# Backbone step on one core: prompt's input projection between the samples' passes, single loads, one-hot gates on the second one-hot

## What is computed

```python
def trunk_layer(x, cvec, ctx_kv, ...):
    shift1, scale1, gate1, shift2, scale2, gate2 = adaln(cvec, w_ada, b_ada)
    h = rmsnorm(x, g_attn) * (1 + scale1) + shift1
    zf, zq, zk, zv, zp = jnp.split(h @ w_in, IN_SPLITS, axis=-1)
    ...
    gf, ga, gp = jnp.split(jax.nn.sigmoid(h @ w_gate + b_gate), N_BRANCHES, axis=-1)
    x = x + gate1 * ((gf * branch_f + ga * branch_a + gp * branch_p) @ w_out)
    h2 = rmsnorm(x, g_ffn) * (1 + scale2) + shift2
    x = x + gate2 * peer_ffn(h2, peer_wq, peer_keys, peer_u, peer_v)

def peer_ffn(h, peer_wq, peer_keys, peer_u, peer_v):
    q = (h @ peer_wq).reshape(B, L, PEER_HEADS, 2, PEER_D_KEY // 2)
    s = jnp.einsum('blhpc,hpnc->blhpn', q, peer_keys)
    sv, si = lax.top_k(s, PEER_TOPK)
    ...
    eid = jnp.take_along_axis(cid, pos, axis=-1)
    act = jax.nn.gelu(jnp.einsum('tkd,td->tk', peer_u[ee], hh))
    return jnp.einsum('tk,tkd->td', gg * act, peer_v[ee])
```

## Time and profile before

| | us |
|---|---|
| median of three runs | 3088.42 (3085.93 to 3094.46) |
| the profiled execution | 3086.08 |
| its span, first to last instruction | 3083.8 |

### The profile page before, as it was taken

One profiled execution on the slowest core, in us unless ns is written; L12 is line 12 of the kernel. 1 busy time (PEld: TensorE's weight loads), 2 busy tenths in 40 slices (PEclk: granted clock), 3 DMA queues, 4 the chain that ended last, 5 costly groups with the idle time before them and its releaser, 6 DMA issues.

```text
span 3083.8 us, 42725 instructions
## 1 busy us (share of the span) xinstructions
PE 2616.6 (85%) x14564; PEld 2042.2 (66%) x14564; DVE 2236.8 (73%) x4292; ACT 1271.1 (41%) x2320; POOL 1282.3 (42%) x966
## 2 busy tenths in 40 slices
PE   5799788856799999999978988884579999999996
PEld 1476654315688888888867666432568888888885
DVE  0335564448699999999993544565868999999998
ACT  0333332106455555455543333211544555555553
POOL 0554621007544444444437455200754444444441
PEclk6799899958999999999989999997899999999998
DMA  9743447595799999999965334663579999999995
GB/s 329 250 150 100 145 168 244 196 336 153 264 366 376 353 375 356 362 376 367 367 248 184 107 135 145 207 227 109 157 260 353 375 362 376 368 373 379 367 377 188
DMA packets 262282, 842.73 MB, mean 273 GB/s; under 512 B 33488, under 2 KB 104848, under 8 KB 224528
## 3 DMA queue, kind: packets, MB, share of 16 engines
q1 hardware_dynamic: 177328, 567.09, 52.0%
q0 software_dynamic: 73728, 268.47, 21.6%
q10 hardware_dynamic: 11104, 5.82, 0.7%
HBM read 805.09 MB, written 39.95 MB: 274 GB/s over the span
## 4 chain that ended last, share of the span: by engine, by line
issue 36%; DVE 27%; DMA 16%; POOL 9%; DVEq 6%; ACT 2%; PE 2%; ACTq 1%; POOLq 1%; SPq 0%; PEldq 0%; PEld 0%
DMA raw<-in_experts 11%; POOL wlo L667 8%; DVE wlo L1992 8%; DVE u L1742 6%; DVEq L2025 5%; DVE u L2003 4%; DVE u L1981 4%; DMA raw<-in_w_ada 3%; DVE u L2013 3%; ACT whi L996 1%; ACTq L1084 1%; DVEq L1987 1%; PE acc L1151 1%; DVE u L1984 1%; DMA raw<-in_peer_wq 0%
## 5 line engine op out<-in xcount | busy, mean ns | idle before, releaser
L673 POOL DMA_INDIRECT u<-in_u_rows,rowid x256 | 474.1, 1852 | 904.4 <-DVE u L1742 716.9
L1992 DVE TENSOR_TENSOR wlo<-raw,whi 128x1024 fp32r<-128x1024 f32 x512 | 624.6, 1221 | 116.8 <-ACT whi L996 80.6
L1502 PE MATMUL aux<-lt_hi,whi 128*128 128x256 f32 x2048 | 606.5, 296 | 71.2 <-DVE wlo L1992 69.4
L996 ACT ACTIVATE whi<-raw 128x1024 fp32r<-128x1024 f32 x512 | 536.5, 1049 | 153.4 <-DMA raw<-in_experts 152.7
L1502 PE MATMUL aux<-lt_hi,wlo 128*128 128x256 f32 x2048 | 584.8, 286 | 0.0
L1502 PE MATMUL aux<-lt_lo,whi 128*128 128x256 f32 x2048 | 584.7, 285 | 0.0
L1502 PEld LDWEIGHTS aux<-lt_hi,whi 128*128 128x128 f32 x2048 | 396.4, 194 | 144.5 <-DVE wlo L1992 128.7
L667 POOL TENSOR_TENSOR wlo<-raw,whi 128x1024 fp32r<-128x1024 f32 x144 | 355.5, 2479 | 267.1 <-ACT whi L822 266.9
L1514 PE MATMUL acc<-whi,bt_hi 128*128 128x512 f32 x1024 | 405.8, 396 | 13.4 <-DVE bt_lo L2022 13.2
L1514 PE MATMUL acc<-wlo,bt_hi 128*128 128x512 f32 x1024 | 404.5, 395 | 0.0
L1514 PE MATMUL acc<-whi,bt_lo 128*128 128x512 f32 x1024 | 401.4, 392 | 0.0
(11 more groups left out here) (211 smaller groups left out, 3841.5 us busy)
## 6 DMA issues: line engine op xcount, KB each, us to landing
raw<-in_experts SPq DMA_DIRECT2D x256, 1024.0 KB
raw<-in_w_ada SPq DMA_DIRECT2D x96, 512.0 KB, 5.4
raw<-in_w_gate SPq DMA_DIRECT2D x48, 1024.0 KB, 5.1
raw<-in_w_in SPq DMA_DIRECT2D x32, 1024.0 KB, 5.3
raw<-in_peer_wq SPq DMA_DIRECT2D x32, 1024.0 KB, 5.1
gmat<-u SPq DMA_DIRECT2D x32, 1024.0 KB, 5.1
z<-gmat SPq DMA_DIRECT2D x32, 1024.0 KB, 8.5
raw<-in_w_out SPq DMA_DIRECT2D x16, 1024.0 KB, 5.0
```

The lines of the kernel that those rows point to most:

```text
L673: pool.indirect_dma_start(UROWS[:, j % UBUF, :], None, a["u_rows"], bass.IndirectOffsetOnAxis(ap=ROWID[:, j:j + 1], axis=0))\
L996: act.activation(whi[:, i % SLOTS], raw[:, i % SLOTS], ACT.Copy).then_inc(expert_hi, 1)
L1502: mm = pe.matmul(b[:, 0:TS], w[:, slot, c * P:(c + 1) * P], x[:, c, :], start=(c == 0 and i == 0), stop=(c == KC - 1 and i == 2))
L1992: dve.tensor_tensor(wlo[:, i % SLOTS], raw[:, i % SLOTS], whi[:, i % SLOTS].bitcast(F32), ALU.subtract)\
```

## The change

**PE order.** The prompt's 8 transposes stand ahead of the samples' wa, in0 between wa and out, in1 between out and q0. The second half of the samples' queries and scores stands beside the prompt's gf (LAST_QUERIES, LAST_SCORES). ACT's copies follow. **Loads.** The prompt's units are loaded one by one, each with its own semaphore. The tables AFTER_SAMPLES and AFTER_PROMPT say which unit frees a slot. The five constant loads stand ahead of the first peer_wq pair. **DVE order.** `chosen(0)`, `indexed(0)` and the second `top_keys` of block 1 stand later among the softmax and merge steps; the products and sums of `indexed(1)` go to POOL as those of block 0 do. **One-hot.** HOT1 is one comparison of eight tokens without the gate; the gate is multiplied into HOT2, by POOL as a second operation, by ACT as the bias and scale of a Relu per token (group 6 alone), by DVE as a second operation (groups 1, 2, 5). SELC gets a fourth row with the negated gate.

```diff
+LAST_QUERIES = {U_GF + 1: (4, 5), U_GF + 2: (6, 7)}
+LAST_SCORES = {U_GF + 4: (0,), U_GF + 5: (1,)}
+AFTER_SAMPLES = {u: U_OUT - SLOTS + u for u in range(SLOTS)}
+AFTER_SAMPLES.update({KC + u: U_Q - SLOTS + u for u in range(SLOTS)})
...
+AFTER_PROMPT = {U_OUT + u: KC - SLOTS + u for u in range(SLOTS)}
+AFTER_PROMPT.update({U_Q + u: 2 * KC - SLOTS + u for u in range(SLOTS)})
...
-BY_ACT = (2, 6)
+BY_ACT = (6,)
...
+                def prompt_units(u0, u1, w, n0):
+                    v = w[bass.ds(l, 1)].rearrange("o (k p) n -> p (o k) n", p=P)
+                    for i, u in enumerate(range(u0, u1)):
+                        if u in AFTER_SAMPLES:
+                            wait_lo(sp, l, AFTER_SAMPLES[u])
+                        else:
+                            sp.wait_ge(raw_used, l * UNITS + u + 1 - SLOTS)
+                        sp.dma_start(raw[:, u % SLOTS, :], v[:, i, n0:n0 + UW]).then_inc(raw_landed[u % SLOTS], 16)
...
                 def pairs(u0, u1, source):
                     for i, u in enumerate(range(u0, u1, 2)):
-                        if u >= SLOTS:
+                        if u in AFTER_PROMPT:
+                            sp.wait_ge(raw_used, l * UNITS + AFTER_PROMPT[u] + 2)
+                        elif u >= SLOTS:
                             wait_lo(sp, l, u - 3)
...
-                            i2 = SELC[:, n // 4, 1, j % GT:j % GT + 1]
-                            x = pool.tensor_scalar(HOT2[:, j % 16, :], iota[:], i2, None, ALU.is_equal)
+                            i2, gg = (SELC[:, n // 4, q, j % GT:j % GT + 1] for q in (1, 2))
+                            x = pool.tensor_scalar(HOT2[:, j % 16, :], iota[:], i2, gg, ALU.is_equal, ALU.mult)
...
-                                act.activation(HOT2[:, 8:12, :], FAR[:], ACT.Relu, bias=one[:], scale=-1.0).then_inc(hot3_ready, 1)
+                                for t in range(4):
+                                    gg, minus = (SELC[:, s, q, 8 + t:9 + t] for q in (2, 3))
+                                    x = act.activation(HOT2[:, 8 + t, :], FAR[:, t], ACT.Relu, bias=gg, scale=minus)
+                                x.then_inc(hot3_ready, 1)
...
+                            dve.tensor_scalar(SELC[:, s, 3], SELT[:, 2, at], -1.0, None, ALU.mult)
...
-                        for j in range(8 * m, 8 * m + 8):
-                            i1, gg = (SELC[:, s, q, j % GT:j % GT + 1] for q in (0, 2))
-                            dve.tensor_scalar(HOT1[:, j, :], iota[:], i1, gg, ALU.is_equal, ALU.mult)
+                        dve.tensor_tensor(HOT1[:, 8 * m:8 * m + 8, :], iota[:].rearrange("p (o n) -> p o n", o=1).to_broadcast([P, 8, P]),
+                                          SELC[:, s, 0, at:at + 8].rearrange("p (t o) -> p t o", o=1).to_broadcast([P, 8, P]), ALU.is_equal)
                         for n in mine:
-                            dve.tensor_tensor(HOT2[:, at:at + 4, :], ...)
+                            for j in range(4 * n, 4 * n + 4):
+                                i2, gg = (SELC[:, s, q, j % GT:j % GT + 1] for q in (1, 2))
+                                dve.tensor_scalar(HOT2[:, j % 16, :], iota[:], i2, gg, ALU.is_equal, ALU.mult)
```

More of the change, by code:

```diff
@@ L126, in _bank_tables @@
     for l in range(DEPTH):
-        for s, blocks in (("s", NB), ("p", 1)):
-            for name, _, _ in PASSES:
-                passed((s, l, name), blocks, "a" if name in BY_ACT_PASSES else "v", name == "out")
+        for s, names in (("s", ("in0", "in1", "gf", "wf", "gp", "wp", "ga", "wa")), ("p", ("in0",)), ("s", ("out",)), ("p", ("in1",)),
+                         ("s", ("q0", "q1")), ("p", ("gf", "wf", "gp", "wp", "ga", "wa", "out", "q0", "q1"))):
+            for name in names:
+                passed((s, l, name), NB if s == "s" else 1, "a" if name in BY_ACT_PASSES else "v", name == "out")
         if l + 1 < DEPTH:
@@ L149, in _bank_tables @@
         small("v", *[("bs", l) + x for i in BESIDE for x in i])
+        small("a", *[("hp", l, g) for g in range(2)])
         small("v", *[("ms", l, k) for k in range(KC)])
@@ L358, in build @@
         rows_stored = sem("rows_stored")
-        raw_landed = [sem("raw_landed0"), sem("raw_landed1")]
+        raw_landed = [sem(f"raw_landed{i}") for i in range(SLOTS)]
         raw_used = sem("raw_used")
@@ L855, in layer @@
                         sigmoid((U_WF, U_WP, U_WA).index(u))
-                for u in range(U_OUT + 2, U_Q + KC + 2):
-                    if u == U_Q + 4:
-                        squares(2 * l + 1)
+                    if u == U_WA:
+                        columns_prompt("hp", 0)
+                hi(U_OUT + 2)
+                hi(U_OUT + 3)
+                passed("p", "in0", zp(0))
+                act.drain().then_inc(zp_ready, 2)
+                for u in range(U_OUT + 4, U_Q):
+                    hi(u)
+                squares(2 * l + 1)
+                for u in range(U_Q, U_Q + 4):
+                    hi(u)
+                passed("p", "in1", zp(D))
+                act.drain().then_inc(zp_ready, 2)
+                for u in range(U_Q + 4, U_Q + KC + 2):
                     hi(u)
@@ L862, in layer, with queries @@
                 act.drain().then_inc(pq_ready, 1)
-                def queries(m):
-                    for j in range(4 * m, 4 * m + 4):
+                def queries(j0, j1):
+                    for j in range(j0, j1):
                         evacuated(PQT[:, 2 * j:2 * j + 2, :].rearrange("p k t -> p (k t)"), ("qs", l, j), HB)
@@ L1917, in layer @@
                 merge_prompt(0, "wf")
-                top_keys(1, 1)
+                chosen(0)
                 gate_prompt(1, "gp")
                 merge_prompt(1, "wp")
+                indexed(0)
+                top_keys(1, 1)
+                gate_prompt(2, "ga")
                 chosen(1)
-                gate_prompt(2, "ga")
                 merge_prompt(2, "wa")
```

165 lines of the change are left out of this document (73 added, 92 removed).

## The result

| | before | after |
|---|---|---|
| median | 3087.18 us (4 runs, 3085.41 to 3094.46) | 3148.16 us (4 runs, 3145.39 to 3150.93) |
| profiled span | 3083.8 us | 3149.1 us |

The ratio is 1.0184 with a 95% interval of 1.0163 to 1.0206. Forecast were 3065 us, within 3022 to 3110: wrong in sign, and outside the range. It came out on the side of rival 1, at a price beyond the part of it that the range held.

A forecast was written before the change was run, and what follows sets the result against it. It took PE, with holes, to carry the prompt stretch, and DVE to bind the one-hot stage, POOL just behind. Profiled 3086.1 - 40.8 (prompt) + 17.4 (one-hot) = 3062.7; the median lies 2.3 above: 3065 us, range 3022 to 3110.

The forecast's parts named there:

- rival 1: One-hot loop: POOL's second operation is dear, 3106 us at x = 0.2; outweighs the gain past 0.13; chance 0.18.
- POOL's second operation: One-hot loop: multiplying by the gate with a second per-partition scalar on POOL, 128 instructions a layer, +5.1 us a layer.
- x: One-hot loop: price of POOL's second operation per instruction, taken as 0.04 us, between bounds 0 and 0.59.
- the blocking: One-hot loop: DVE's two-operand comparisons lengthen POOL instructions they meet, up to 0.92 each, four a pass; +3.6 us a layer.
- the prompt's missing gain: Samples' output projection to the end of the prompt's sub-layer 1: 20.4 us saved a layer, 40.8 for both.
- The shift of the samples' passes: PE, in0 and in1 among samples' passes: out begins 12.8 later, q0 24 later, gf 27 earlier.
- DVE's chain: Ahead of the prompt's out: DVE ends last, at about 526, PE idle some 15; gives back 3 of 21 us.
- "indexed(1)" on POOL at nothing: Prompt's part: moving these products to idle POOL takes 9 us of DVE out of the next wait, costed at nothing.
- Single loads: Prompt's out, q0 and q1: loading per unit removes half the waits for w_out and w_q, 2.4 us a layer.
- the row of the gate and merge: DVE's chain in the prompt's part: a gate and merge step counted as 4.0 us busy, twice.
- the upper bound of the gain: Prompt's part, both layers: 2 x 24 us, with all 4.8 of stalls gone and 4 fewer of drains and waits.

The follow-up runs named there:

- a4: Kernel before with only the one-hot part, but HOT1 made by 32 one-operation tensor_scalars per pass instead of four long comparisons: 1.0065 of the kernel before.
- a3: Kernel before with only the one-hot part, but POOL's instruction with one operation again, its groups left without the gate: 1.0083 of the kernel before.
- b1: a1 with the five constant loads behind the last loads of q1 instead of ahead of the first peer_wq pair: 0.9909 of the kernel before.
- c1: b3 with the prompt's in0 and in1 behind q1 again, as in the kernel before: 0.9866 of the kernel before.
- b3: a1 with DVE work wanted only in the one-hot stage put behind what PE waits for, ACT's and POOL's orders following: 0.9830 of the kernel before.
- c2: Kernel before with single loads for the prompt's units and nothing else: 0.9874 of the kernel before.
- a1: The whole change without its one-hot part, HOT1 and HOT2 made as in the kernel before: 0.9956 of the kernel before.
- b2: a1 with the products and sums of indexed(1) back on DVE, as in the kernel before: 0.9917 of the kernel before.
- b4: a1 with the edits of b1 and b3 together: 0.9794 of the kernel before, 0.9805 when repeated.

## Why the prediction was wrong, step by step

**POOL's second operation: the step that failed.** x was taken as 0.04 on the ground that an operation on loaded elements is far nearer to nothing than to a second pass. It is 0.19: 128 x 0.191 = 24.4 a layer in place of 5.1. The row that it leaned on, DVE's two operations "at its usual pace", had no row with one operation beside it. a4 has both in one pass, first one operation, then two:

```profile
748.84 1.66 DVE L1986 TENSOR_SCALAR u<-iota,u 128x128 f32<-128x128 f32 x8 [0.37 <-PE aux L1492]
750.41 1.29 DVE L1990 TENSOR_SCALAR u<-iota,u 128x128 f32<-128x128 f32 x4
```

The eight with one operation begin 0.196 apart (1.57 / 8, and the median of all of them), those with two 0.257: on DVE, too, the second operation with its scalar adds a third, as 0.19 does to POOL's 0.60. The range stopped at x = 0.2 with the blocking held at its forecast size. The estimate that the prediction made from the Trainium skill's page "GPSIMD Engine Reference", section "Performance pitfalls for Q7 kernels", 0.085, was nearer, but the measured price is more than twice that.

**The blocking** was the right mechanism, one size too small: 1.04 a meeting and not 0.92. The forecast had 3.6 a layer for it; a3, which has the blocking and not the second operation, shows 13.5 and 11.6. The larger meetings make up 3.8 of that difference (8 passes x 4 x 0.12); the rest, in the longer passes towards the ends of the stage, stays open. Both prices fall on the same engine: the prediction saw POOL at 13.2 beside 12.78, and with x at 0.19 everything more on POOL is paid in full, so that passes of some 17 follow.

**Rival 1** named the cause and the point at which it decides (0.13). It was given 0.18. Its own sum at x = 0.19 would be 3088 - 41 + 56 = 3103; that 3148 was measured is due to the prompt's missing gain and to the blocking beside it.

**The shift of the samples' passes.** in0 pushed out 14.9 later and both passes pushed q0 29.1 later (table: 22.4 - 7.5 and 74.6 - 45.5), as much as the 28.5 that they last. From the span's start, as the forecast counts, it is 14.1 and 28.3; forecast were 12.8 and 24. The loads that used to run ahead in the holes now start when the prompt's units leave the ring: q0's first pair was issued at 338.7, 26.5 us ahead of q0, before, and at 379.9, 13.6 ahead of it, now. The congested constants account for 4.6 of the wait ahead of q0 (b1), but not for the late gf: with them gone hardly a mark moved. Behind a drained ring POOL makes its low halves without a pause, and DVE's turning of the tiles, which PE needs for the next unit, is held. DVE between the third and the fourth unit of q0 in the kernel before, then in after, and POOL there:

```profile
373.11 0.55 DVE L1672 TENSOR_SCALAR z<-aux,modc 128x256 f32<-128x256 f32 x1 [1.90 <-PE aux L1247]
373.57 0.29 DVE L1664 CAST lt_hi<-z 128x256 fp32r<-128x256 f32 x1
373.77 0.42 DVE L1666 TENSOR_TENSOR lt_lo<-z,lt_hi 128x256 fp32r<-128x256 f32 x1
...
401.75 0.55 DVE L1702 TENSOR_SCALAR z<-aux,modc 128x256 f32<-128x256 f32 x1 [0.86 <-PE aux L1279]
402.21 2.32 DVE L1694 CAST lt_hi<-z 128x256 fp32r<-128x256 f32 x1
404.44 2.57 DVE L1696 TENSOR_TENSOR lt_lo<-z,lt_hi 128x256 fp32r<-128x256 f32 x1
...
401.98 7.28 POOL L686 TENSOR_TENSOR wlo<-raw,whi 128x1024 fp32r<-128x1024 f32 x3 [1.57 <-ACT whi L842]
```

The cast goes from 0.29 to 2.32 and the subtraction from 0.42 to 2.57. From the first unit of q0 on, the next four begin 5.0, 3.0, 5.6 and 4.6 apart here, against 4.6, 3.0, 3.0 and 3.0 before; in c1, where no prompt units go through the ring ahead of out and q0, they are 5.6, 3.1, 3.0 and 3.0. With these waits gf came 17.3 earlier and not 27.

**DVE's chain.** That it ends last was right, and PE's wait too (15.72, forecast some 15). But it starts from gf, so the 10 us lost above returned at its end, and the chain took 75.4 from its first search to 540.0, not 71. The working did count the searches in this chain; what neither it nor the change asked is whether they must stand in it. In the kernel before, DVE's searches ran beside the prompt's in0 and in1 (columns as in the earlier trace rows):

```profile
427.80:467.30 39.50, 31.88 (x64) 12.99 (x64) 28.12 (x150) 3.29 (x7) 9.90 (x3) 0.91 0.65 227
```

28.1 us of DVE work stood under that stretch of PE. Taking PE's work away from it left DVE's behind, ahead of a merge that PE waits for. The change's order on DVE put all of it there; b3 shows that 17 us a layer of it had somewhere else to go. c2 is the sharpest form of this: its gf begins 17.5 later than a1's, and its prompt's out 3.4 earlier.

**"indexed(1)" on POOL at nothing** was wrong. POOL was idle, as the prediction said, but its product held DVE's normalising instruction for 4.2 in each layer, and layer 1's one-hot stage became 2.0 longer (b2).

**Single loads** were under-counted. The 2.4 a layer were for the prompt's out, q0 and q1, where c2 shows 6.1 and 5.0; another 9.9 and 7.6 came ahead of the prompt's out, for which nothing was counted: the waits for w_gate (4.2 in the kernel before) and for w_attn, w_fourier and w_pool (3.9) don't stand in the sum. In the change from the prompt's out on 1.9 and -0.4 are left, the wait of 9.40 having taken 4.2 back.

Two of the sum's smaller readings are off as well: the row of the gate and merge reads 3.90, not 4.0, and the upper bound of the gain doesn't follow from its terms (18 + 4.8 + 4 is 26.8, not 24). Neither decides anything here.

The sum by measured terms: the prompt's part 6.4 in place of 40.8, the one-hot stage 75.8 in place of 17.4. These two terms miss by 34.4 and 58.4; of the second, x alone makes 38.6.

**A version that beats both** came out of it: b4, the prompt part with DVE's deferrable work and the constants behind what PE waits for, and the one-hot loop as before, 0.979 and 0.981 in two comparisons.

## What to carry to other kernels

An engine that stands just behind the one that binds (POOL at 10 of 12.8) has no room for an operation whose price no row shows: measure that price before giving the engine more work. A row of another engine is no price by itself either: what the second operation adds is seen only beside a row without it. When work is moved off a stretch, ask what another engine did under its cover, and where that now ends; here DVE's searches had to be moved too. And look at what a hole is used for before filling it: here loads ran ahead in it, and with other work there the wait came back at the next start (5.10 and 7.50).

## What the runs showed of the hardware

- POOL and DVE hold each other in both directions. DVE's 128x1024 comparison with two operands in SBUF makes a POOL tensor_scalar of 0.79 last 1.83; POOL's tensor_tensors hold DVE's 128x1024 tensor_scalar (0.75 to 4.97), its 128x256 cast (0.29 to 2.32) and its 128x256 subtraction of two tiles (0.42 to 2.57). The Trainium skill, page "SBUF — State Buffer", section "Who interferes with whom", has a port pair that the two engines share as an exclusive lock, which DVE's copies, casts and tensor_scalars can take in their 2-port modes, and has DVE instructions with two inputs in SBUF contend with a GpSimd instruction that reads SBUF. The trace agrees in that a cast, a tensor_scalar and a subtraction of two tiles were held; in which mode they ran it doesn't show.
- The comparison itself isn't held by a POOL tensor_scalar that began before it, as a lock for the whole of that instruction would have it. In after, 61 of the 64 comparisons begin while one runs, and all of them take 1.22 to 1.29; nine of them begin within 0.09 us of its start, and there it is POOL's instruction that is stretched, to 1.83 to 1.86. In a3 six that begin within 0.18 us take 1.27 to 1.37, the longest there are.
- A second operation with a second per-partition scalar on 128x128 elements costs POOL 0.19 (597 to 788 ns) and DVE 0.06 (0.196 to 0.257 us from start to start, a4): a third on either. Operation and scalar weren't separated.
- Beside DVE's tensor_scalars POOL's two-operation instruction takes 0.86 in place of 0.79; its one-operation instruction keeps 0.60.
